# Experts taken in pairs, the scatter moved later, and low halves of the weights shared out between two engines

## What is computed

```
cap = 2 * T // 16                       # 64 latent, 32 context tokens per expert
aff = softmax(h @ w_router); vals, idx = top_k(aff.T, cap)
xg  = h[idx]                            # (16, cap, 1024)
hid = silu(xg @ w1) * (xg @ w3)         # three 1024 x 1024 matrices per expert
y   = (hid @ w2) * vals
out = zeros.at[idx].add(y)              # scattered back, added over experts
```

## Time and profile before

| | before |
|---|---|
| median of 3 runs (lowest to highest) | 3895.54 us (3892.78 to 3901.08) |
| the profiled execution: time, span | 3890.03 us, 3888.4 us |
| PE busy | 3477.1 us (89%) |
| DVE busy | 2320.3 us (60%) |
| ACT, POOL busy | 1587.3 us (41%), 781.9 us (20%) |
| DMA, mean over the span | 163 GB/s |

### The profile page before, as it was taken

How to read it: one execution, slowest core, us unless ns; L and a number is a source line. 1 busy time by engine, 2 the same in 40 slices (tenths; PEclk the granted TensorE clock), 3 DMA queues, 4 the chain that set the end, 5 groups by cost and what they waited for, 6 DMA issues and landing times.

```text
span 3888.4 us, 50468 instructions
## 1 busy us (share of the span) xinstructions
PE 3477.1 (89%) x19428; PEld 2716.2 (70%) x19428; DVE 2320.3 (60%) x3486; ACT 1587.3 (41%) x2055; POOL 781.9 (20%) x480
## 2 busy tenths in 40 slices
PE   6989899899999879999997299998999959999994
PEld 4978578888887756666664288678766746666663
DVE  2685741511112659999997584833232459999996
ACT  3213752411110236666663222744211136666662
POOL 2001012221210113233231200122222112323231
PEclk8989999999999889999998599998999979999997
DMA  7232133022122438889886122121222229999993
GB/s 240 98 131 93 36 107 120 12 71 87 60 82 77 141 123 310 311 305 311 308 305 256 56 80 83 50 89 43 71 88 75 98 77 327 328 332 324 330 330 146
DMA packets 331924, 632.85 MB, mean 163 GB/s; under 512 B 14526, under 2 KB 104910, under 8 KB 325358
## 3 DMA queue, kind: packets, MB, share of 16 engines
q1 hardware_dynamic: 309056, 557.88, 41.4%
q0 software_dynamic: 22704, 72.68, 5.6%
HBM read 614.00 MB, written 16.50 MB: 162 GB/s over the span
## 4 chain that ended last, share of the span: by engine, by line
PE 63%; DVE 13%; issue 9%; ACT 6%; DMA 6%; POOL 2%; DVEq 0%; ACTq 0%; POOLq 0%; SPq 0%
PE ps L845 43%; PE ps L1245 10%; ACT hx L1514 2%; DMA raw<-in_w_exp_down 2%; DMA raw<-in_w_exp_gate 2%; PE ps L970 2%; PE ps L1002 2%; DVE part L2066 2%; POOL hx L792 1%; DVE area L1668 1%; PE ps L988 1%; DVE hx L2066 1%; ACT area L1366 1%; ACT area L1294 1%; PE ps L990 1%
## 5 line engine op out<-in xcount | busy, mean ns | idle before, releaser
L845 PE MATMUL ps<-hx,part 128*128 128x384 f32 (+2 forms) x4704 | 931.1, 356 | 26.2 <-DVEq L528 21.9
L845 PEld LDWEIGHTS ps<-hx,part 128*128 128x128 f32 x4704 | 832.0, 189 | 114.5 <-DVEq L528 23.6
L1245 PE MATMUL ps<-part,hx 128*96 128x512 f32 x3072 | 760.0, 398 | 24.6 <-DVE part L2066 17.5
L2066 DVE TENSOR_TENSOR part<-raw,part 128x2048 fp32r<-128x2048 f32 x256 | 616.0, 2407 | 90.2 <-ACT part L1514 89.7
L1245 PEld LDWEIGHTS ps<-part,hx 128*96 128x96 f32 x3072 | 493.7, 163 | 235.6 <-DVE part L2066 35.8
L1514 ACT ACTIVATE part<-raw 128x2048 fp32r<-128x2048 f32 x256 | 489.9, 1915 | 200.2 <-PE ps L1245 178.3
L514 POOL TENSOR_TENSOR part<-raw,part 128x2048 fp32r<-128x2048 f32 x52 | 238.1, 4579 | 856.1 <-ACT part L511 828.8
L1245 PE MATMUL ps<-hx 128*96 128x512 f32 x1536 | 377.5, 394 | 2.0 <-DVE hx L2066 1.4
L845 PE MATMUL ps<-part,hx 128*128 128x256 f32 (+2 forms) x2208 | 315.4, 305 | 17.3 <-DVEq L528 15.5
L1245 PEld LDWEIGHTS ps<-hx 128*96 128x96 f32 x1536 | 246.7, 161 | 110.0 <-POOL hx L792 4.4
L845 PEld LDWEIGHTS ps<-part,hx 128*128 128x128 f32 x2208 | 295.1, 197 | 34.8 <-DVEq L528 16.2
(11 more groups left out here) (252 smaller groups left out, 3722.8 us busy)
## 6 DMA issues: line engine op xcount, KB each, us to landing
raw<-in_w_exp_gate SPq DMA_DIRECT2D x128, 1024.0 KB, 5.2
raw<-in_w_exp_up SPq DMA_DIRECT2D x128, 1024.0 KB, 5.5
raw<-in_w_exp_down SPq DMA_DIRECT2D x128, 1024.0 KB, 5.6
raw<-in_w_mod SPq DMA_DIRECT2D x48, 1024.0 KB, 7.6
raw<-in_w_in SPq DMA_DIRECT2D x44, 1024.0 KB, 5.3
raw<-in_w_gate SPq DMA_DIRECT2D x32, 1024.0 KB, 8.0
area<-in_bias POOLq DMA_DIRECT2D x32, 512.0 KB, 4.1
raw<-in_w_branch SPq DMA_DIRECT2D x16, 1024.0 KB, 7.3
```

Of the source, the lines that this page charges most:

```text
L845: last = mm(dst, a, b, start=i == 0, stop=i == len(pairs) - 1)
L1245: last = mm(ps[0:CAP, bank, :], x, y, start=kh == 0 and a == 0, stop=kh == 1 and a == len(pairs) - 1)
L2066: V.tensor_tensor(expert_part(s, 1), src, expert_part(s, 0).bitcast(f32), ALU.subtract).then_inc(S("split_v"), 1)
```

## The change

- **Experts in pairs.** Latent rows of expert `j` = 0 stand on partitions 0 to 63 and those of `j` = 1 on 64 to 127, in one `put`, `y_hi`, `y_lo`. One scatter then serves two experts: 8 latent pieces, 2 matmuls each, over 128 rows, after blocks 1 to 8 of the next pair's first expert. Its wait for `y_lo` moves from behind block 0 to behind block 1.
- **Context rows.** They stand twice in `xg` (columns 64 to 127 for `j` = 0, 0 to 63 for `j` = 1). The high part of the result is kept on 32 of these partitions and the low part on the other 32, in `y_ctx`. So one matmul with `put_ctx` adds high and low of two experts; its 4 pieces follow blocks 1, 3, 5, 7 of the second expert (layer 0 alone).
- Results, hidden and its turned form are 128 wide in place of 96.
- **Halved low parts.** Of blocks 1, 3, 5, 7 (`G_HALVES`) DVE makes the first half of the rest and POOL the second. DVE makes all of every other block, 5 no longer being POOL's alone. TensorE and SP wait for both halves.
- `y_hi` and `y_ctx` are two instructions on ACT for one, `y_lo` and the low of `y_ctx` two on DVE (layer 0 alone). ACT clears `y_hi` and `y_lo` at the start of a stage. The last scatter goes over four banks. SP's loop is written out.

```diff
-G_SPLITS = (5,)
+G_HALVES = (1, 3, 5, 7)
+def scatters(j, b, per):
+    if j == 0:
+        return range(b - 1, b) if 1 <= b <= 2 * TL else range(0)
+    c = 2 * TL + b // 2
+    return range(c, c + 1) if b % 2 and c < per else range(0)
...
+rows_of = [(slice(0, CAPL), slice(CAPL, P)), (slice(CAPL, P), slice(0, CAPL))]
+high_of = [slice(CAPL, CAPL + CAPC), slice(0, CAPC)]
+low_of = [slice(CAPL + CAPC, P), slice(CAPC, CAPL)]
...
 POOL:
+moves = [(rows_of[j][0], src[:, :, 0:CAPL]), (high_of[j], src[:, :, CAPL:CAP]),
+         (low_of[j], src[:, :, CAPL:CAP])][:3 if full == NT else 1]
 (one copy to xg_hi and one subtraction to xg_lo for each of them)
-for s in (EXP_BLOCKS * j + b for b in G_SPLITS):
+for s in (EXP_BLOCKS * j + b for b in G_HALVES):
     pool.wait_ge(S("split_h"), ...)
+    nc.gpsimd.tensor_tensor(expert_part(s, 1)[:, 2:4, :], raw ... [:, 2:4, :],
+                            expert_part(s, 0)[:, 2:4, :].bitcast(f32), ALU.subtract).then_inc(S("split_g"), 1)
...
 TensorE:
+if t < TL:
+    last = passes(ps[:, bank, :], [(put[rows, t * P:(t + 1) * P], y[rows, at]) for y in (y_hi, y_lo)])
+else:
+    last = mm(ps[:, bank, :], put_ctx[rows, ...], y_ctx[rows, at], start=True, stop=True)
...
-if b == 0:
+if b == 1:
     pe.wait_ge(*S("e_yL", l).at(i * 4 + 2 * j + 2))
+for c in scatters(j, b, per):
+    pe.wait_ge(*S("e_acc", l).at(i * per + (c + 1)))
+    scatter(c, 4, slice(0, P))
...
 DVE:
+ks = slice(0, 2 if s % EXP_BLOCKS in G_HALVES else 4)
+V.tensor_tensor(expert_part(s, 1)[:, ks, :], src[:, ks, :], expert_part(s, 0)[:, ks, :].bitcast(f32),
+                ALU.subtract).then_inc(S("split_v"), 1)
+lows = [(rows_of[j][0], y_lo, y_hi), (low_of[j], y_ctx, y_ctx)][:2 if ctx_out else 1]
```

More of the change, by code:

```diff
@@ L80, in expert_block, with halves_before, scattered @@
     return "w_exp_down", b % 2 * NCH, (b - 8) // 2
-def rest_rank(s):
+def halves_before(s):
     e, b = s // EXP_BLOCKS, s % EXP_BLOCKS
[L88 to L101, removed]
+    return NG * e + sum(g < b for g in G_HALVES)
+def scatters(j, b, per):
[3 more added lines that the diff above has]
+    return range(c, c + 1) if b % 2 and c < per else range(0)
+def scattered(c):
+    return (c // TL, c % TL) if c < 2 * TL else ((c - 2 * TL) // TC, TL + (c - 2 * TL) % TC)
 def ring_plan(l):
@@ L1204, in _, with scatter @@
                 st.leave()
-                ncomb = 2 * full
+                per = 2 * full
                 n += EXP_BLOCKS * E
                 pe.drain().then_inc(*S("e_comb", l).by(1))
[L1210 to L1216, removed]
+                def scatter(c, bank, rows):
+                    half, t = scattered(c)
+                    at = slice(half * NCH, (half + 1) * NCH)
+                    if t < TL:
+                        last = passes(ps[:, bank, :], [(put[rows, t * P:(t + 1) * P], y[rows, at]) for y in (y_hi, y_lo)])
+                    else:
+                        last = mm(ps[:, bank, :], put_ctx[rows, (t - TL) * P:(t - TL + 1) * P], y_ctx[rows, at], start=True, stop=True)
+                    last.then_inc(*S("e_comb", l).by(1))
                 def turn_hidden(half, count):
@@ L1257, in _ @@
                 pe.wait_ge(*S("e_yL", l).at(2 * E + 2))
-                for c in range(ncomb):
-                    scatter(c, E * ncomb + 1)
+                for c in range(per):
+                    pe.wait_ge(*S("e_acc", l).at(E // 2 * per + 1 + max(c - 3, 0)))
+                    scatter(c, c % 4, slice(0, P) if c < 2 * TL else rows_of[1][1])
                 st.leave()
@@ L1502, in _ @@
                 st.leave()
-                m = CAP if ctx_out else CAPL
+                per = 2 * full
                 r0 = B_EXP[l]
@@ L1535, in turn @@
                             act.wait_ge(*S("e_val", l).at(i * 2 + (j + 1)))
[L1536 to L1538 removed]
+                            act.wait_ge(*S("e_comb", l).at(i * per + ((per if j else 2 * TL) + 1)))
+                            for r, y in list(zip(rows_of[j], (y_hi, y_ctx)))[:2 if ctx_out else 1]:
+                                last = fn(y[r, half * NCH:(half + 1) * NCH], ps[r, 5 + half, :], ACT.Copy, scale=val[r, 0:1])
+                            last.then_inc(*S("e_yH", l).by(1))
                 for s in range(AHEAD):
                     hi(0, s)
+                for y in (y_hi, y_lo):
+                    for half in range(2):
+                        last = fn(y[:, half * NCH:(half + 1) * NCH], consts[:, 0:NCH], ACT.Copy, scale=0.0)
+                last.then_inc(*S("y_zero", l).by(1))
                 with turns(act, E // 2 - 1) as i:
@@ L2130, in _ @@
                 turn(E // 2 - 1, True)
-                for c in range(ncomb):
-                    add(c, E * ncomb)
+                for c in range(per):
+                    add(c, c % 4, E // 2 * per)
                 st.leave()
```

134 lines of the change are left out of this document (66 added, 68 removed).

## The result

The changed kernel took 3875.53 us (median of 4 runs, 3872.74 to 3879.54), the kernel before 3898.31 us on the same chip: a ratio of 0.9946, 95% interval 0.993 to 0.9961. That is 15 to 27 us faster, 22.8 by the medians, where the forecast had 38. Its profiled execution took 3872.74 us (span 3870.8), 17 less than that of before.

The account below looks back on a forecast made before the run. It took DVE and the port it shares with POOL as the bound. +1 - 22 - 10 - 5 - 8 + 6 = -38 on the profiled 3890.0 gave 3852, with 5.5 for the median 3858 us; range 3800 to 3915.

Parts of the forecast that it names:

- start, layers 0 and 1: Start of each stage: block 1 waits for slot loads and POOL's half, +3 us a layer.
- steady, layer 0: Layer 0 experts: mean 41.9 us against 41.83, bound by DVE and the port, +1 us in all.
- steady, layer 1: Layer 1 experts: mean 37.6 us against 38.94, -22 us in all.
- last interval, where the last weights come: Last expert: POOL issues layer-norm loads later, so fewer meet the weights; -4 us a layer, between 0 and -8.
- last scatter: Last scatter of each layer: with four banks only DVE paces it, 0.64 us a piece; -10 and -5.
- The port: DVE with two SBUF inputs and POOL block each other for whole instructions; blocked 5.9 to 8.4 us an expert.
- TensorE's pace: Rival: POOL's halves fit into DVE's PSUM work, 36.9 and 36.5 us an expert, about -137, 3759 us; 12%.
- The walk through the blocks: One pair followed: DVE blocked at blocks 3, 5, 7, 1.7 or 2.3 us each; layer 0 experts 42.3 and 41.5.
- TensorE waiting longest for POOL's half at block 1, up to 3 us: Block 1: POOL's half stands behind `put` and slot loads; costs 1.4 us an expert in layer 0, 1.7 in layer 1.
- DVE is never idle in it: Layer 0 experts: bound by DVE and the port without idle time, TensorE having nearly 5 us to spare.
- The slower rival: Rival: the port hides less; half of POOL's unpaid port time paid gives +77, 3935 us; 20%.
- ACT would not wait for weights in the steady part: Steady part of the expert stages: ACT waiting for weights there would show the forecast wrong; no size given.

Follow-up runs that it names:

- g3: e1 plus four half-size POOL subtractions an expert into memory that nobody reads: 3988.85 us, ratio 1.0241.
- e2: Changed kernel with POOL's halves of blocks 3, 5, 7 alone, DVE making all of block 1's rest: 3869.15 us, ratio 0.992.
- e3: Changed kernel with POOL's slot loads behind its half of block 1, all halves kept: 3872.75 us, ratio 0.9934.
- g2: The changed kernel itself run once more, unedited, as neighbour of g1: 3871.19 us, ratio 0.9938.
- h1: e1 with POOL's next-stage loads held back until TensorE has used block 7 of the last expert: 3804.49 us, ratio 0.9764.
- e1: Changed kernel with no halves on POOL, DVE making every rest whole: 3825.8 us, ratio 0.9808.
- e4: Changed kernel with the old split of rests, POOL making all of block 5 and no halves: 3861.17 us, ratio 0.9903.
- g1: f4 run once more, the same kernel with ten extra matmuls: 3872.62 us, ratio 0.9939.
- f4: Changed kernel with ten extra matmuls filling TensorE's wait at block 1 of each expert in layer 0: ratio 0.9942.

## Why the prediction was right in its direction and too large in its size

Each term of its sum, read from the two profiled executions between the same rows (POOL's first cast, `put`, the first operation of the norm or the end):

| term | predicted | measured |
|---|---|---|
| start, layers 0 and 1 | +3, +3 | +3.1, +3.8 |
| steady, layer 0 | +1 | +6.9 |
| steady, layer 1 | -22 | -12.4 |
| last interval, where the last weights come | -4, -4 | -6.6, -8.0 |
| last scatter | -5, -10 | -2.3, -10.3 |
| sum | -38 | -25.8 |

The front part, whose code is the same, took 8 us longer in this execution (6 ahead of layer 0's stage and 2 ahead of layer 1's), which leaves 17.6 of the span; the medians, 22.8 apart, are nearer to the stages. The steady parts, of which the forecast expected 21, gave 5.5; that the whole came as near as it did is partly luck, since the last expert gave more than its term.

- **The port.** Right, and shown: DVE's halves cost 2.25 on average, 3.42 behind POOL; TensorE's pace is not reached; g3 measures the block by itself. The walk through the blocks was right in part: in the experts I followed, the half of block 3 is blocked each time in layer 0 (3.4 us), those of blocks 5 and 7 in some experts and not in others (1.2 to 3.4). Adding up what DVE's rests in layer 0 take beyond 1.22 and 2.28, DVE is blocked 6.0 us in a first expert and 6.4 in a second where the clock stays up, for 6.8 and 8.4 in the sum.
- **"TensorE waiting longest for POOL's half at block 1, up to 3 us", from `put` and the slot loads.** Right in place and length (3.0 to 3.2 in layer 0, up to 1.8 in layer 1). Its price of 1.4 and 1.7 an expert can't be read alone. Without the half at block 1 (e2) the wait goes and 1.1 of DVE's work comes back: -0.3 and -0.6 by my numbers, -0.17 and -0.24 measured, which is no more than one kernel's executions differ by (0.11 and 0.29). With the loads behind it (e3) layer 0 gains 0.38 only.
- **Steady, layer 0: the failed step is its first experts.** The walk gave 42.3 and 41.5. The intervals are 41.1 to 41.3 for the second expert of a pair (once 42.2), and for the first 42.2 in one case and 43.3 to 43.8 in six. In these six the twelve matmuls of block 1 took 4.3 to 4.6 us; in the one of 42.2 they took 3.0. g2 repeats it, with five slow ones at 43.3 to 43.8 and two at 42.2 and 42.3 (the row under this item is block 1 in one of the two: 3.02 us behind a wait as long as the others). With the wait filled and the clock at 1.00 all of them fell to 42.2 or 42.3. So what failed is "DVE is never idle in it", with "TensorE has nearly 5 us to spare": behind the slow block DVE stood idle 1.7 to 4.4 us of a first expert, against 0.8 where the clock stayed up. A clock that falls in the wait was in no term of the sum. It costs 0.5 to 0.6 us an expert, all of the excess; without it the walk's 41.9 stands beside 41.72. In second experts the same slow block cost nothing (41.1) unless it took 5.49 us (42.2).

```profile
1783.11 3.02 PE L1253 MATMUL ps<-part,hx 128*128 128x512 f32 x12 [3.16 <-POOL part L798]
```

- **Steady, layer 1: mis-sized.** Predicted 39.2 and 35.9, measured 39.9 to 40.5 and 36.0 to 36.7. In h1, where TensorE is busy 98%, the experts take 38.4 and 34.4: my 37.8 for the first was too low, since 0.2325 a matmul leaves no room for the small waits behind scatters. In a first expert of the changed kernel DVE is blocked 6.5 us, where the sum had 5.9, and idle 1.1, where it had none; these experts exceed the walk by 0.7. TensorE waits 1.4 us an expert for POOL's half (14.2 in ten), but without that wait (e2) layer 1 isn't clearly shorter, so it isn't what the excess hangs on. Weights that come late lengthen some second experts from 36.0 to 36.7. (Before, the mean was 39.07, not 38.94, for one expert of 40.57 with late weights.)
- **Last weights: right mechanism, and more than forecast.** POOL's halves delay the next stage's loads: they start 18.9 us behind the fifteenth placement of layer 0 before and 26.1 after, and ACT's waits for weights in the last expert of layer 0 fall from 12.6 us to 2.3. The later they start, the shorter the last interval of layer 0, if not to the last us: 47.3 to 48.3 us where they start up to 18.9 behind (e1, e4, before), 43.6 to 44.0 at 23.6 to 23.8 (g1, f4, e2), 39.6 to 41.7 at 24.2 to 26.1 (e3, g2, changed). With nothing else changed, h1 moved the start from 3.8 to 26.8 and the interval from 47.3 to 35.8. Of the 6.6 and 8.0 us in the table, 0.5 and 2.6 are what every second expert saves; the weights' share is 6.1 and 5.4, so 11.5 in place of eight. That is nearly half of the change's gain in the profiled stages, and it comes from a side effect.
- **Last scatter.** Layer 1 right. In layer 0 the adds themselves fell, from 12.6 to 7.8, but `y_lo` in four parts came later (first add 6.1 behind `put`, in place of 4.2), and the norm waited 0.8 for POOL, which the loads hold up.
- **Rivals.** TensorE's pace did not come. The slower rival (half of the unpaid port paid) neither; g3 says that 40 to 50% of port time is hidden when DVE is full.
- **Signs.** That ACT would not wait for weights in the steady part held in layer 0 alone; in layer 1 it waited 15 us in 400, in pieces of up to 1.8. The kernel before waited there too (5.7 us, up to 2.6): "once, for 1.0 us" was read in layer 0. TensorE was busy 90.6% in layer 0, not under 90%.

## What to carry to other kernels

When two engines share a lock, as DVE and POOL do here, moving a piece from one to the other can pay only as far as the first has work outside the lock; what the lock alone costs is measured with the same piece into memory that nobody reads. Split a change into its parts on both kernels; here the pairs gave 10 thousandths, the halves took 4 of them back, and leaving POOL out altogether would have given 19. A total that doesn't move can hide two effects: the filled wait gained 7 us in one stretch and lost half of it in the next. And look at what an engine's queue issues when it becomes free: loads of the next stage that start early can cost the last round of this one more than an edit in the steady part brings.

## What was not expected of the hardware

After a wait of TensorE of about 3 us the granted clock fell or did not. In steady layer 0 of the changed kernel it fell behind eleven of fifteen such waits at block 1 (3.0 to 3.2 us each): the twelve matmuls then took 4.3 to 5.5 us, in place of 3.0 behind the other four, though the waits are of the same length. In 1616.0 to 1619.8, behind the wait of 3.13, the mean granted clock was 0.59, so most of that stretch ran at the 1.2 GHz level; in 1620 to 1625, with TensorE busy throughout, it was 0.99, nearly all at 2.4 GHz. Over 400 us it read 0.97, and 1.00 once ten matmuls stood in the wait. In layer 1 of g2 waits of 1.76 or 1.77 us were enough in three first experts (the row of one is below; the clock was 0.62 in 3443 to 3447), while in the changed kernel's first execution waits of 1.6 to 1.8 us lowered nothing in seven first experts.

```profile
3442.93 4.62 PE L1253 MATMUL ps<-part,hx 128*128 128x512 f32 x12 [1.77 <-POOL part L798]
```

The Trainium skill (TensorE: Matmul & The Clock Gate, "Part 1: The HAM clock gate") says that the throttled state is the default and that activity releases it; the trace agrees in that the clock fell behind idle time and came back under work.

POOL's slot loads stayed at 0.52 to 0.57 us each, beside DVE's rests too, so the prediction's worry that they would starve did not come true. The Trainium skill (SBUF — State Buffer, "SBUF: two separate sides") describes that starving for a DVE in a 2-port mode; no run here shows that these subtractions of two SBUF operands run in such a mode.
